# Stick-breaking attention without mask products: the causal mask moved from TensorE to GpSimd selects on the sigmoids' results

## The reference, cut to what matters

```python
z = jnp.einsum('bqhd,bkhd->bhqk', q_blk, k).astype(jnp.float32) * scale
before = k_pos[None, :] < q_pos[:, None]
log_keep = jnp.where(before, jax.nn.log_sigmoid(-z), 0.0)
tail = lax.cumsum(log_keep, axis=3, reverse=True) - log_keep
w = jnp.where(before, jnp.exp(jax.nn.log_sigmoid(z) + tail), 0.0)
```

## Time and profile before

| | |
|---|---|
| median of 3 runs | 833.79 us (833.06 to 834.5) |
| the profiled execution | 833.79 us, its span 832.1 us |
| PE busy | 815.5 us, 98% of the span |
| DVE busy | 600.2 us, 72% |
| ACT busy | 401.7 us, 48% |
| POOL busy | 102.5 us, 12% |
| slots 4 to 7 | begin at 190.2, 219.5, 248.8 and 278.1 us |

### The profile page before, as it was taken

The page is one execution under the profiler, slowest core; times in us unless marked ns, Lnnn a source line. Parts: engine busy times, 40 slices in busy tenths (PEclk is TensorE's granted clock), DMA queues, the critical chain, the costliest instruction groups (busy, mean ns, idle before and its releaser), DMA issues.

```text
span 832.1 us, 11742 instructions
## 1 busy us (share of the span) xinstructions
PE 815.5 (98%) x3855; PEld 677.3 (81%) x3855; DVE 600.2 (72%) x849; ACT 401.7 (48%) x560; POOL 102.5 (12%) x87
## 2 busy tenths in 40 slices
PE   5999999999999999999999999999999999899998
PEld 4888888888888888888888888888888887678886
DVE  5525888867668675555554578878777878798797
ACT  6434776655545544434341454333333333555663
POOL 2100010000000060000000003333233233200000
PEclk9999999999999999999999999999999999999999
DMA  6333242222222222333366523666655663466455
GB/s 207 103 102 89 71 120 77 83 70 68 84 76 69 71 77 88 95 96 101 88 222 245 182 83 91 202 202 202 200 186 194 201 199 130 147 208 211 149 185 173
DMA packets 130110, 113.26 MB, mean 136 GB/s; under 512 B 6068, under 2 KB 109464, under 8 KB 128672
## 3 DMA queue, kind: packets, MB, share of 16 engines
q1 hardware_dynamic: 129264, 110.64, 42.2%
q0 software_dynamic: 672, 2.12, 1.0%
q10 hardware_dynamic: 144, 0.13, 0.0%
HBM read 99.21 MB, written 13.65 MB: 136 GB/s over the span
## 4 chain that ended last, share of the span: by engine, by line
PE 93%; DVE 3%; DMA 1%; issue 1%; ACT 1%; SPq 1%; DVEq 0%; ACTq 0%
PE ps L1456 29%; PE ps L1457 28%; PE ps L1458 28%; PE ps L1550 2%; PE ps L1540 2%; PE ps L1565 1%; PE ps L1564 1%; DMA w_raw<-in_w_in_dram 1%; PE ps L1718 0%; DVE out_sb L1441 0%; SPq L280 0%; DVE conv_out L1299 0%; DVE conv_in L1308 0%; ACT conv_out L811 0%; PE ps L1510 0%
## 5 line engine op out<-in xcount | busy, mean ns | idle before, releaser
L1456 PE MATMUL ps<-h_lo,w_hi 128*128 128x512 f32 x704 | 277.6, 394 | 4.0 <-DVE w_lo L891 3.2
L1457 PE MATMUL ps<-h_hi,w_hi 128*128 128x512 f32 x704 | 274.8, 390 | 0.0
L1458 PE MATMUL ps<-h_hi,w_lo 128*128 128x512 f32 x704 | 274.7, 390 | 0.0
L891 DVE TENSOR_TENSOR w_lo<-w_raw,w_hi 128x1024 fp32r<-128x1024 f32 x119 | 150.0, 1261 | 133.0 <-ACT w_hi L516 78.2
L516 ACT ACTIVATE w_hi<-w_raw 128x1024 fp32r<-128x1024 f32 x96 | 101.7, 1060 | 195.9 <-PE ps L1458 195.8
L1456 PEld LDWEIGHTS ps<-h_lo,w_hi 128*128 128x128 f32 x704 | 132.5, 188 | 32.2 <-DVE w_lo L891 3.6
L1458 PEld LDWEIGHTS ps<-h_hi,w_lo 128*128 128x128 f32 x704 | 132.6, 188 | 27.8
L1457 PEld LDWEIGHTS ps<-h_hi,w_hi 128*128 128x128 f32 x704 | 132.7, 188 | 26.6
L494 POOL TENSOR_TENSOR sg<-sg,conv_out 128x512 f32<-128x512 f32 x22 | 38.4, 1744 | 322.7 <-ACT sg L816 322.7
L1302 DVE SCALAR_TENSOR_TENSOR conv_out<-conv_in,par,conv_out 128x512 f32<-128x512 f32 x44 | 50.2, 1141 | 5.5 <-DVE conv_out L1299 0.2
L510 ACT ACTIVATE w_hi<-w_raw 128x1024 fp32r<-128x1024 f32 x24 | 25.4, 1059 | 54.4 <-PE ps L1458 54.2
(11 more groups left out here) (221 smaller groups left out, 1301.8 us busy)
## 6 DMA issues: line engine op xcount, KB each, us to landing
w_raw<-in_w_in_dram SPq DMA_DIRECT2D x104, 256.0 KB, 3.1
w_raw<-in_w_up_dram SPq DMA_DIRECT2D x88, 256.0 KB, 3.2
raw_t<-in_w_down_dram SPq DMA_DIRECT2D x11, 1024.0 KB, 8.8
down_sums<-t_sum SPq DMA_DIRECT2D x11, 1024.0 KB, 5.7
w_raw<-in_w_down_dram SPq DMA_DIRECT2D x33, 256.0 KB, 3.1
w_raw<-down_sums SPq DMA_DIRECT2D x33, 256.0 KB, 3.8
w_raw<-in_w_out_dram SPq DMA_DIRECT2D x16, 256.0 KB, 3.3
w_raw<-down_sums SPq DMA_DIRECT2D x22, 128.0 KB, 2.9
```

The source lines that it names most:

```text
L891: v.tensor_tensor(w_lo[:, slot, :], w_raw[:, slot, :], r32(w_hi[:, slot, :]), ALU.subtract)\
L1456: mm3(dst, l_hi, r_lo, start=start, stop=False, **kw)
L1457: mm3(dst, l_hi, r_hi, start=False, stop=False, **kw)
L1458: return mm3(dst, l_lo, r_hi, start=False, stop=stop, **kw)
```

## The change

The eight mask products of each B slot are left out, with their two matrices and what builds them. The first score product of each block starts the accumulation instead. After ScalarE has written keep[h], GpSimd selects on its four diagonal blocks of 128 x 128: where the key isn't before the query it writes 1. After ScalarE has written pa[h] it does the same with 0. VectorE's scan waits for keep_masked instead of keep_done, and its weights wait for beta_masked instead of beta_done.

```diff
@@ gpsimd, at the start @@
-            pool.memset(ident_b[:, :], 0.0)
-            pool.memset(causal_b[:, :], 0.0).then_inc(const_step, 1)
-            pool.wait_ge(const_step, 2)
-            pool.affine_select(out=ident_b[:, :], in_=ident_b[:, :], compare_op=ALU.not_equal, fill=1.0, base=0,
-                               pattern=[[-1, P]], channel_multiplier=1)
-            pool.affine_select(out=causal_b[:, :], in_=causal_b[:, :], compare_op=ALU.is_gt, fill=MASKED, base=0,
-                               pattern=[[-1, P]], channel_multiplier=1)
+            pool.wait_ge(const_step, 1)
@@ gpsimd, after the bias loads @@
+            def keep_earlier_keys(buf, fill):
+                for qt in (3, 2, 0, 1):
+                    c = S_OFF[qt] + qt * P
+                    last = pool.affine_select(out=buf[:, c:c + P], in_=buf[:, c:c + P], compare_op=ALU.is_gt, fill=fill,
+                                              base=0, pattern=[[-1, P]], channel_multiplier=1)
+                return last
+            for s in range(4):
+                for h in range(2):
+                    pool.wait_ge(keep_done, s * 2 + (h + 1))
+                    keep_earlier_keys(keep[h], 1.0).then_inc(keep_masked, 1)
+                    pool.wait_ge(beta_done, s * 2 + (h + 1))
+                    keep_earlier_keys(pa[h], 0.0).then_inc(beta_masked, 1)
@@ vector: stick_scan, stick_weights @@
-                d.wait_ge(keep_done, hh - 7)
+                d.wait_ge(keep_masked, hh - 7)
-                d.wait_ge(beta_done, hh - 7)
+                d.wait_ge(beta_masked, hh - 7)
@@ tensor: scores @@
-                if masks:
-                    for qt in (3, 2, 1, 0):
-                        c = S_OFF[qt] + qt * P
-                        for h in range(2):
-                            mm3(flat[h][:, c:c + P], ident_b[:, :], causal_b[:, :], start=qt != 0, stop=False,
-                                skip_group_check=True)
-                            last = mm3(flat[h][:, c:c + n], a_q[r, 0, q], a_k[r, 1, 0:n], start=i == 0 and not masks,
-                                       stop=i == 2, skip_group_check=masks)
+                            last = mm3(flat[h][:, c:c + n], a_q[r, 0, q], a_k[r, 1, 0:n], start=i == 0, stop=i == 2)
```

More of the change, by code:

```diff
@@ L109, in build @@
         masked = sb("masked", [P, 2, HD])
-        ident_b = sb("ident_b", [P, P], mybir.dt.bfloat16)
-        causal_b = sb("causal_b", [P, P], mybir.dt.bfloat16)
         inv = sb("inv", [P, 3, 16])
@@ L199, in build @@
         keep_done, beta_done, scan_done = sem("keep_done"), sem("beta_done"), sem("scan_done")
+        keep_masked, beta_masked = sem("keep_masked"), sem("beta_masked")
         suffix_init = sem("suffix_init")
@@ L1521, in _, with scores @@
                 values(N_VB, V_B_BANKS, u)
-            def scores(s, attn):
+            def scores(s):
                 flat = [ps[:, HEAD[h]:HEAD[h] + 3, :].rearrange("p b c -> p (b c)") for h in range(2)]
-                masks = attn == "B"
-                if masks:
-                    for qt in (3, 2, 1, 0):
-                        c = S_OFF[qt] + qt * P
-                        for h in range(2):
-                            mm3(flat[h][:, c:c + P], ident_b[:, :], causal_b[:, :], start=qt != 0, stop=False,
-                                skip_group_check=True)
                 for qt, c, n in segs():
@@ L1566, in output, with slot_begin @@
                 last.then_inc(pv_done, 1)
-            def slot_begin(s, attn):
+            def slot_begin(s):
                 pe.wait_ge(qk_lo_ready, s * 2 + 2)
@@ L1575, in slot_begin @@
                     pe.wait_ge(o_sum_ready, s * 2)
-                scores(s, attn)
+                scores(s)
                 if isinstance(s, int) and s == 0:
@@ L1585, in slot_a @@
                 t = s * 2 + 2
-                slot_begin(s, "A")
+                slot_begin(s)
                 tile_of(b, 0, PROJ[0])
@@ L1611, in slot_b @@
                 b = s * 4 + N_SLOT
-                slot_begin(s, "B")
+                slot_begin(s)
                 tile_of(b, 0, PROJ[0])
```

## The result

The changed kernel takes 836.42 us (median of 12 runs, 835.15 to 837.67), the kernel before, run beside it, 833.96. The ratio is 1.0031 with a 95% interval of 1.0023 to 1.0040. The direction was right, the size was not: +2.5 us (profiled execution against profiled execution 837.07 - 833.79 = +3.3) instead of +5.85. The time lies in the forecast's range. By the time alone it is nearer to the rival without blocking (834.5 us) than to the forecast (839.6); what decides between them is the trace and experiment e3.

The account below looks back on a forecast made before the run. TensorE, busy throughout slot 4, was taken as the bound, with VectorE's queue having no slack at tile b+2's low weights. Slots 4 to 7 summed 2.47 + 1.35 + 1.35 + 0.68 = +5.85 on 833.79, giving 839.6 us, range 834.0 to 843.5.

Parts of the forecast that it names:

- the rival without blocking: Scans don't block GpSimd's selects, which run hidden under them; D is 1.12, sum +0.66, 834.5 us; chance 0.27.
- The gain on TensorE: Start of slots 4 to 7: dropping eight mask products saves 0.46 us a slot, 1.84 us in four.
- The places: TensorE waits at head 0's transposes and tile b+2's low weights, the tightest; slots cost +2.47, +1.35, +1.35, +0.68 us.
- D: Delay of VectorE's queue at the low weights of tile b+2, forecast as 2.47 us.
- its room: What a slot hides of D: nothing in slot 4, 0.80 + 0.32 in slots 5 and 6, 1.79 in slot 7.
- the prediction's own formulas: Slot costs: D in slot 4, D - 0.80 - 0.32 in slots 5 and 6, D - 1.79 in slot 7.
- The first term, 1.12 for keep's selects: Before the first scan: four selects of keep[0] take 1.04 us, the second handoff 0.08, so it starts 1.12 later.
- The mechanism of the rest: Selects beside VectorE's scans and weights share a port; whichever starts first blocks the other for its whole instruction.
- The queued scans: Rival: VectorE's four queued scans go ahead of waiting selects; D 3.2, sum 8.8 us, 842.5 us; chance 0.15.
- I take 0.10: Each select falling between two VectorE instructions pushes the next back 0.10 us, between bounds of 0 and 0.25.
- the fourth of pa: pa[0]'s last select, which head 0's weights must wait for, costs 0.25 us with its handoff.
- The bound that the prediction had worked out with 0.05 a select: Lower variant: 0.05 a select and 0.20 for the fourth's handoff give D 1.87, sum 3.4, 837.2 us.

Follow-up runs that it names:

- e3: Changed kernel with its sixteen selects a slot on a dead buffer and VectorE waiting for none, mask left out: 833.13 us, ratio 0.9993 to the kernel before.
- e1: Changed kernel without any selects, so neither mask products nor selects, causal mask left out: 832.22 us, ratio 0.9983 to the kernel before.
- e4: Changed kernel with raw_lo and tile b+2's low weights ahead of the second scan in slots 4 to 6: 835.39 us, ratio 1.0019 to the kernel before.
- e5: Changed kernel with the sigmoid table load moved to right behind slot 3's last exponentials: 835.04 us, ratio 1.0012 to the kernel before.
- e2: Changed kernel with six dead-buffer memsets between keep and scan instead of selects, nothing for beta, mask left out: 833.92 us, ratio 1.0002 to the kernel before.
- e6: Changed kernel with three diagonal blocks in one select, eight selects a slot instead of sixteen: 836.78 us, ratio 1.0035 to the kernel before.
- e7: Changed kernel with the first scan starting after keep's first select, last two selects of each buffer swapped: 836.53 us, ratio 1.0031 to the kernel before.
- e8: Changed kernel with the moves of e4, e5 and e7 together: 833.01 us, ratio 0.9988 to the kernel before.

## Why the prediction was right or wrong

**The gain on TensorE: right.** 0.46 us a slot was forecast from the earlier trace rows; the slots of e1 show 0.45 or 0.46 where there is room.

**The places: right.** The low weights of tile b+2 as the tightest place, slot 4 as the worst slot because of the table load, and the order slot 4, 5 and 6, 7 are borne out by e4 and e5. The net loss of a slot as D less its room works as forecast. With D = 1.87 put in, the prediction's own formulas give 1.87, 0.75, 0.75 and 0.08, and 1.81, 0.84, 0.53 and -0.07 were measured. They are off by up to 0.22. Two small things are in that: keep[0] moved up by 0.42 us in slots 5 and 6 and 0.34 in slot 7, not by 0.32 and 0.23, and in slot 5 D was 2.15, so that slot's good fit is in part luck.

**The first term, 1.12 for keep's selects: nearly right.** It is 1.18. Four selects took 1.03 (forecast 1.04), and the handoff to GpSimd 0.15, not 0.08.

**The mechanism of the rest: right, and here the rivals fell.** The scans do block GpSimd's selects and are blocked by them: a select beside a scan lasts up to 1.3 us, and e3 has the effect without any wait. By the rule of the Trainium skill in "SBUF — State Buffer", under "SBUF: two separate sides", two SBUF inputs are enough for that, and the trace agrees (scans of 3.12 instead of 2.97). The same section has it that a VectorE instruction with two SBUF inputs doesn't contend with a GpSimd instruction which only writes; e2's memsets agree (0.94 us for six beside a scan, 0.93 alone). (The prediction speaks of three VectorE operations with two SBUF inputs; its rows show two, L891 and L1302.) The queued scans did not keep the way either: the waiting select got its turn after each of them.

**What failed: the size of D.** The step was "I take 0.10" for each of eleven selects, with 0.25 more for the fourth of pa, 1.35 in all; 0.69 was measured. Two parts of it were wrong. A select of 128 columns that waits for a VectorE instruction costs the next one some 0.04 to 0.07 us (e3: 0.60 for thirteen), and only the one that got in first cost 0.13. That most of a short select fits into a gap between two VectorE instructions is argued from e6, where the larger one costs 0.28, and not shown by itself. And the fourth select of pa did not come after the last scan: pa was ready just as the scan started, its first select went ahead, and the four were done at 199.53, before the scan's end at 199.81: the first scan and pa's selects cost 0.27 instead of 0.55, and the eight others 0.42 instead of 0.80. Because D's excess of 0.6 counts in all four slots, it became 2.4 us of the sum, and with that most of the difference between 5.85 and the 3.11 of the profiled slots. The bound that the prediction had worked out with 0.05 a select, D = 1.87 and +3.4 us, came nearest. That it hits D to the hundredth is luck: its 1.12 was 1.18, and its 0.75 was 0.69.

The medians differ by 2.5 us where the slots of the profiled executions give 3.1; the interval of the ratio (1.9 to 3.3 us) holds both.

## What to carry to other kernels

A wait that is hidden at its own place is paid at the tightest place behind it in the same queue: list for each result of the queue how long before its use it is ready, and compare the smallest of these with the whole delay that the change puts at the queue's head. Then look whether other orders of the queue give room before giving the change up: here the same change is 0.3% slower or 0.26% faster by the place of three VectorE instructions and one table load. GpSimd as a helper beside VectorE is dear in waiting (its handoffs, its own work in the chain and its blocked reads), and cheap in what it takes from VectorE as long as its instructions are short; a signal for a first part helps little if the part's user then blocks the helper.

## What the runs showed of the hardware

A select of 128 x 128 float32 starts every 0.25 us, like one of bfloat16 (1.03 us for four; the prediction only assumed this, though the kernel before has a float32 select of 0.29 us too, L438), and one of 128 x 384 takes 0.52.

In every kernel with selects on keep, one slot's first select started 0.51 or 0.52 us after keep's end, all others 0.14 or 0.15. With sixteen selects a slot it is slot 5, the second one (225.18 to 225.69 in the changed kernel), and with e6's eight a slot it is slot 6, the third. In e3, which has another program around its selects, and in e2 with memsets, it isn't there. In both cases it is the first select behind sixteen others, and e7 and e8, which change what VectorE does, have it at the same place; so it seems to go by the place in GpSimd's program. That it is the fetching of instructions is a guess; no run was made for it, and the cause stays open. It costs its slot 0.2 to 0.3 us where there is no room (slot 5 against slot 6: 0.31 in the changed kernel, 0.26 in e4).
